# A two-layer diffusion block with sixteen experts: rotary query columns in one tile, earlier expert loads, and a first block of slots made from the counts alone

## What is computed

```
cq, ckv, kr, bq, bk, bv, dq, dk, dv, u = split_in(modulate(rms_norm(x)) @ w_in)
# MLA: 4 heads, a query is 64 plain and 32 rotary columns
qa = (rms_norm(cq) @ w_uq).reshape(B, L, 4, 64 + 32)
qa = concat([q_nope, apply_rope(q_rope)])              # latent tokens are roped, context tokens not
ka = concat([k_nope, broadcast(apply_rope(kr))])       # one rotary key for all heads
oa = softmax(qa @ ka * MLA_SCALE) @ va
ob = windowed softmax with a sink (bq, bk, bv)         # "swa"
oc = (softmax(dq1 @ dk1) - lam * softmax(dq2 @ dk2)) @ dv   # "diff"
od = means over 2/4/8/16 positions (u), times pool_w   # "pool"
x  = x + gate * rms_norm(concat(oa, ob, oc, od) @ w_out)
# experts: top-1 of 4 groups, top-2 of its 4 experts
h  = modulate(rms_norm(x)); e1, e2, w1, w2 = route(h @ router_gw, h @ router_ew)
x  = x + gate * rms_norm(sum_e w_e * (silu(h @ gate_e) * (h @ up_e)) @ down_e)
```

## Time and profile before

| | us |
|---|---|
| median of the runs | 1171.84 |
| the three runs | 1171.67, 1171.84, 1176.56 |
| the profiled execution's own time | 1174.54 |
| its span in the profile | 1172.7 |
| PE busy | 912.5 (78%) |
| DVE busy | 363.0 (31%) |
| ACT busy | 266.9 (23%) |
| POOL busy | 174.1 (15%) |

### The profile page before, as it was taken

One profiled execution on the slowest core, in us unless ns is written; L12 is line 12 of the kernel. 1 busy time (PEld: TensorE's weight loads), 2 busy tenths in 40 slices (PEclk: granted clock), 3 DMA queues, 4 the chain that ended last, 5 costly groups with the idle time before them and its releaser, 6 DMA issues. The chain is left out here.

```text
span 1172.7 us, 23091 instructions
## 1 busy us (share of the span) xinstructions
PE 912.5 (78%) x8840; PEld 570.6 (49%) x8841; DVE 363.0 (31%) x909; ACT 266.9 (23%) x728; POOL 174.1 (15%) x256
## 2 busy tenths in 40 slices
PE   3999998999995899989973399988994873764570
PEld 2454644556454566656642366746643542432240
DVE  1100057568335111111110664376624110100013
ACT  4121034556232011101100521035521000000001
POOL 0010015000021222112211230032012110100011
PEclk9999999999996899999997699999995998977796
DMA  9972334660357799999997995130068999999963
GB/s 377 347 262 101 144 144 148 231 234 1 137 187 306 258 412 409 410 411 411 411 411 296 386 345 205 33 125 31 8 251 316 404 408 410 410 411 410 410 272 139
DMA packets 97332, 323.03 MB, mean 275 GB/s; under 512 B 11946, under 2 KB 22964, under 8 KB 90996
## 3 DMA queue, kind: packets, MB, share of 16 engines
q1 hardware_dynamic: 70528, 279.19, 60.4%
q0 software_dynamic: 9600, 31.81, 7.8%
q10 hardware_dynamic: 17140, 11.13, 3.0%
HBM read 309.58 MB, written 18.81 MB: 280 GB/s over the span
## 5 line engine op out<-in xcount | busy, mean ns | idle before, releaser
L851 PE MATMUL psum<-weights,lat 128*32 128x256 f32 x2688 | 177.0, 418 | 99.3 <-DMA weights<-in_exp_w_gu_dram 61.9
L851 PEld LDWEIGHTS psum<-weights,lat 128*32 128x32 f32 x2688 | 107.5, 119 | 164.0 <-issue 130.7
L1662 DVE STREAM_TRANSPOSE lat<-lat 128x256 f32<-128x256 f32 x66 | 29.4, 446 | 352.3 <-PE psum L851 341.1
L529 PE MATMUL psum<-hT,weights 128*128 128x512 f32 (+1 forms) x336 | 121.1, 519 | 3.5 <-ACT lat L1025 1.9
L1201 ACT ACTIVATE lat<-psum 128x128 f32<-128x128 f32 x64 | 17.7, 277 | 356.0 <-PE psum L851 352.5
L529 PEld LDWEIGHTS psum<-hT,weights 128*128 128x128 f32 x336 | 64.4, 193 | 56.8 <-issue 48.4
L864 PE MATMUL psum<-weights,lat 128*32 128x256 f32 x1344 | 85.0, 391 | 5.4 <-issue 4.7
L1908 POOL DMA_INDIRECT lat<-h_rows,slot_col x68 | 66.5, 978 | 54.2 <-POOL slot_col L1905 52.2
L1433 DVE TENSOR_REDUCE st<-psum 128x1 f32<-128x512 f32 (+1 forms) x96 | 56.5, 599 | 41.5 <-PE psum L647 20.6
L864 PEld LDWEIGHTS psum<-weights,lat 128*32 128x32 f32 x1344 | 55.2, 114 | 27.0 <-issue 6.9
L1905 POOL COPY slot_col<-slots 128x1 int32 (+1 forms) x68 | 12.4, 183 | 364.3 <-DVE lat L1662 347.1
(11 more groups left out here) (269 smaller groups left out, 1226.6 us busy)
## 6 DMA issues: line engine op xcount, KB each, us to landing
weights<-in_exp_w_gu_dram SPq DMA_DIRECT2D x44, 2048.0 KB
weights<-in_ada_w_dram SPq DMA_DIRECT2D x24, 2048.0 KB, 8.5
weights<-in_exp_w_down_dram SPq DMA_DIRECT2D x22, 2048.0 KB
hT<-in_exp_w_gu_dram SPq DMA_DIRECT2D x10, 2048.0 KB
R<-in_exp_w_gu_dram SPq DMA_DIRECT2D x10, 2048.0 KB
spare_w<-in_exp_w_down_dram SPq DMA_DIRECT2D x10, 2048.0 KB
weights<-in_w_in_dram SPq DMA_DIRECT2D x6, 2048.0 KB, 15.0
weights<-in_w_out_dram SPq DMA_DIRECT2D x4, 2048.0 KB, 9.6
```

What stands on the lines that cost most here:

```text
L529: mm = nc.tensor.matmul(t[:, lo:hi], w[:, k, col:col + P], hT[:, k, lo:hi], start=(k == 0), stop=(k == KD - 1))
L851: mm = nc.tensor.matmul(gu_ps[BLK * j:BLK * j + BLK, 0:256], xgT[:, k, :], w[:, k % 4, j, :, :, :], start=(k == 0), stop=(k == KD - 1), sk ...
L1662: nc.vector.transpose(xgT[:, :, :].rearrange("p k s -> p (k s)"), xg[par]).then_inc(x_ready, 1)
```

## The change

Four things are changed.

1. The columns of `w_uq` are loaded in another order: the four heads' 64 plain columns side by side (two heads per tile, `qn`), and all heads' 32 rotary columns in one tile of 128 (`qr`). So PE makes three tiles of 128 columns instead of four of 96; one rotation, one product with cosines and one `rope` do for the four heads, with the constants of "diff" (same dimension); and the "mla" constants are gone (the constants' load shrinks from 3,265 to 2,629 columns). The load of `w_uq` becomes four DMAs, with pieces of 64 or 32 columns, 256 or 128 bytes, where one DMA had pieces of 1,536 bytes. ACT copies the parts of the tiles to the heads, and also takes over the four `kr` copies from DVE. The first scores wait for `qr_out` and `kr_out`.
2. In layer 0 `ROPED_LATE` has the units 4, 8, 12 and 16 instead of 3 to 6, and the split of the context half of `dq` (four copies with three heads zeroed) is done by ACT in `project`, so DVE's split has 256 columns instead of 512.
3. SP's loads of the first three experts: some pieces of experts 0 and 1 are issued during the mixing, as their places fall free (`bv` and `dk` change places in `W[0]` for that, and `dg` gets a buffer of its own in layer 1). Expert 2's `lo` now waits for the stored rows as well.
4. The first block's slots need no list: the tokens of expert 0 with rank 0 to 31 are found from "rk" alone (`hot0` on DVE, "s0" on PE, `slot_col` on DVE), and POOL issues gather 0 by it, ahead of its wait for `slots`.

The diff, cut to its core:

```diff
-        ROPED_LATE = {3: "dq0", 4: "dk0", 5: "dq1", 6: "dk1"}
+        ROPED_LATE = [{4: "dq0", 8: "dk0", 12: "dq1", 16: "dk1"}, {3: "dq0", 4: "dk0", 5: "dq1", 6: "dk1"}]
...
 # PE, latent_projections
-                for h in range(HEADS):
-                    t = take("qa", L, h)
+                for col, job in ((2 * P, ("qr", L)), (0, ("qn", L, 0)), (P, ("qn", L, 1))):
+                    t = take(*job)
                     for j in range(2):
-                        mm = nc.tensor.matmul(t[0:MLA_QK, 0:nq], w_uq[:, j, h * MLA_QK:(h + 1) * MLA_QK], cq[:, j, 0:nq],
-                                              start=(j == 0), stop=(j == 1))
+                        mm = nc.tensor.matmul(t[:, 0:nq], w_uq[:, j, col:col + P], cq[:, j, 0:nq], start=(j == 0), stop=(j == 1))
...
-                for name in ("qa0", "qa1", "qa2", "qa3"):
-                    x, kind, lo, hi = ROPES[L][name]
-                    rotate(S, L, name, x, kind, lo, hi)
+                x, kind, lo, hi = ROPES[L]["qr"]
+                rotate(S, L, "qr", x, kind, lo, hi)
...
 # PE, mix
-                            pe.wait_ge(*at("roped", L, f"qa{h}"))
+                            pe.wait_ge(*at("qr_out", L, h))
                             pe.wait_ge(*at("ka", L, h))
                             pe.wait_ge(*at("kr_out", L, h))
...
 # PE, route, between "rk" and "st"
+                pe.wait_ge(*at("hot0", L))
+                t = take("s0", L)
+                for i in range(nt):
+                    for a in range(QUADS):
+                        mm = nc.tensor.matmul(t[BLK * a:BLK * a + BLK, 0:4], hot0[:, i, :], ones[:, 0:4],
+                                              start=(i == 0), stop=(i == nt - 1), skip_group_check=True)
...
 # ACT's queue in layer 0, small_weights
-            eng.dma_start(w_uq[:, :, :], A["mla_w_uq"][L].rearrange("(j p) n -> p j n", p=P)).then_inc(*mark(S, by=16))
+            for j in range(2):
+                src = A["mla_w_uq"][L].rearrange("(j p) (h c) -> p j h c", p=P, h=HEADS)[:, j, :, :]
+                for at_col, lo, hi in ((0, 0, MLA_NOPE), (2 * P, MLA_NOPE, MLA_QK)):
+                    dst = w_uq[:, j, at_col:at_col + HEADS * (hi - lo)].rearrange("p (h c) -> p h c", h=HEADS)
+                    eng.dma_start(dst, src[:, :, lo:hi]).then_inc(*mark(S, by=16))
...
 # ACT, project
-                    copy(S, dqs[L][:, j, 0, 0:nq], (f"dq{j}", L), nq, scale=DIFF_SCALE, keys=[("tile", L, f"dq{j}")])
+                    src = read(act, f"dq{j}", L)
+                    for c in range(4 if nq > SEQ else 0):
+                        a(dqs[L][:, j, c, SEQ:nq], src[:, SEQ:nq], ACT.Copy, scale=C("quarter_scaled")[:, c:c + 1])
+                    copy(S, dqs[L][:, j, 0, 0:SEQ], (f"dq{j}", L), SEQ, scale=DIFF_SCALE, keys=[("tile", L, f"dq{j}")])
...
 # ACT, latent_projections
-                for h in range(HEADS):
-                    copy(S, qas[L][0:MLA_QK, h, 0:nq], ("qa", L, h), nq, hi=MLA_QK, scale=MLA_SCALE, keys=[("tile", L, f"qa{h}")])
+                src = read(act, "qr", L)
+                for h in range(HEADS if nq > SEQ else 0):
+                    a(qas[L][64:96, h, SEQ:nq], src[MLA_ROPE * h:MLA_ROPE * (h + 1), SEQ:nq], ACT.Copy, scale=MLA_SCALE)
+                a(qr[:, 0:SEQ], src[:, 0:SEQ], ACT.Copy, scale=MLA_SCALE).then_inc(*mark(S, ("read", "qr", L), ("tile", L, "qr")))
+                for j in range(2):
+                    src = read(act, "qn", L, j)
+                    for b in range(2):
+                        a(qas[L][0:MLA_NOPE, 2 * j + b, 0:nq], src[64 * b:64 * b + 64, 0:nq], ACT.Copy, scale=MLA_SCALE)
...
+                for name, dst, src in (("kr", kas[L], [kr[64:96, :]] * HEADS), ("qr", qas[L], [qr[MLA_ROPE * h:MLA_ROPE * (h + 1), 0:SEQ] for h in range(HEADS)])):
+                    act.wait_ge(*at("roped", L, name))
+                    for h in range(HEADS):
+                        a(dst[64:96, h, 0:src[h].shape[1]], src[h], ACT.Copy).then_inc(*mark(S, (name + "_out", L, h)))
...
 # DVE, route
+                tt_(rs[:, 38, 0:nt], C(f"token{L}")[:, 0:nt], chosen[:, 0:nt], ALU.mult).then_inc(*mark(S, ("token0", L)))
...
                 t = read(v, "rk", L)
+                step(tt_(hot0[:, 0:nt, :], t[:, 0:nt].unsqueeze(2).to_broadcast([P, nt, BLK]),
+                         C("count")[:, 0:BLK].unsqueeze(1).to_broadcast([P, nt, BLK]), ALU.is_equal))
+                v.wait_ge(*at("token0", L))
+                step(tt_(hot0[:, 0:nt, :], hot0[:, 0:nt, :], rs[:, 38, 0:nt].unsqueeze(2).to_broadcast([P, nt, BLK]), ALU.mult), ("hot0", L))
...
                 step(nc.vector.tensor_tensor_scan(start32[:, :], ones[:, 0:17], nb32[:, :], 0.0, ALU.mult, ALU.add))
+                first = read(v, "s0", L)
+                ts(slot_col[:, 0:1], first[:, 0:1], C("quad"), None, ALU.add).then_inc(*mark(S, ("read", "s0", L), ("slot0", L)))
...
 # SP, ahead of a layer's experts
-                sp.wait_ge(*at("filled", "o", L, len(units(L)) - 1))
+                last, per = len(units(L)) - 1, len(units(L)) // 3
+                if L:
+                    sp.wait_ge(*at("used", item_no[("ada", 1, 11)]))
+                    load_piece(L, 1, 1, "hi")
+                sp.wait_ge(*at("filled", "o", L, per - 1))
+                load_piece(L, 0, 0, "lo")
+                sp.wait_ge(*at("filled", "o", L, 2 * per - 1))
+                load_piece(L, 0, 0, "hi")
+                if L == 0:
+                    sp.wait_ge(*at("filled", "s", L, last, 1))
+                    load_piece(L, 1, 1, "dn")
+                sp.wait_ge(*at("filled", "o", L, last))
                 sp.wait_ge(*at("filled", "pool", L, 1))
-                for piece in PIECES:
-                    load_piece(L, 0, 0, piece)
+                load_piece(L, 0, 0, "dn")
                 for n in (hi - 2, hi - 1):
                     sp.wait_ge(*at("used", n))
-                for piece in PIECES:
+                for piece in (("lo", "dn") if L else ("lo", "hi")):
                     load_piece(L, 1, 1, piece)
                 sp.wait_ge(*at("filled", "lg", L, tiles(L) - 1))
-                load_piece(L, 2, 2, "lo")
                 for tt in range(tiles(L)):
                     sp.wait_ge(*at("h_stored", L, tt))
+                load_piece(L, 2, 2, "lo")
```

67 lines of the change are left out of this document (40 added, 27 removed).

## The result

The changed kernel ran in 1167.77 us (median; 1161.24 to 1170.35), the kernel before, beside it, in 1173.86 (1171.15 to 1176.56). The ratio is 0.9946, 95% interval 0.9932 to 0.996: faster by 0.5%, some 6 us, where 11.2 us, 1.0%, had been forecast. The profiled execution took 1167.77 us, its span in the profile is 1165.9 us.

What follows compares the result with a forecast made beforehand. DMA engines bound the expert stages, where only the stream's start counts; elsewhere the PE, DVE, ACT chain does. Terms 1.8 − 6.0 − 1.3 − 1.9 − 3.8 = −11.2 from the median 1171.84 gave 1160.6 us, range 1154.5 to 1169.5.

Steps and rivals of the forecast that it cites:

- (a): Layer 0's load of w_uq: its small pieces on ACT's queue delay ACT by 5.4 us; cost +1.8 us, bounds 0 and +4.1.
- (b): Layer 0's mixing: PE's idles of 1.40 and 3.67 us and the slow clock behind go; −6.0 us, bounds −2 and −8.
- the mixing gives most of it back: Rival: gap before first scores lowers the clock, ACT's copies delay first units; (b) and (d) shrink to about −3; chance 0.24.
- (d): Start of layer 1's mixing: DVE takes first maxima at 774.0 instead of 775.96; −1.9 us, bounds 0 and −3.
- (c): Layer 0's handover: early gather 0 lets the first block and the saturated stream start earlier; −1.3 us, bounds −0.5 and −1.6.
- (e): Layer 1's handover: store and gathers land sooner, expert 2's hi and dn go out earlier; −3.8 us, bounds 0 and −5.
- (f): Early loads of expert pieces during the mixing: worth 0 by themselves, counting only through (e).
- Slower: Rival: w_uq's small pieces pass ACT's queue at only 60 per us, PE late by 26.3 us; net +13.3, 1185; chance 0.05.
- the store isn't held by the load: Rival, layer 1's handover: engines serve queues in turn, so moving lo doesn't help; (e) only −1.5, total −8.9, 1163.0; chance 0.08.

## Why the prediction was right or wrong

**What bounds the kernel**: right. The share of the DMA engines stayed at 1.02 to 1.03 and 407 GB/s in both expert stages, and what counted was when they begin.

**(a) +1.8**: the time right, in part by luck. At the squares it is 1.8 us between the means of the two kernels' two traces each, with PE's wait at 0.5 to 2.35. But ACT's delay, which I took as 5.4 us against a slack of 3.6, is 3.6 in the mean over all traces; only the earlier trace rows, whose first copy at 59.50 is one of the earliest, makes it 5 to 6, and the second trace of the kernel before has that copy at 62.92 and 0.75 us of wait already. So delay and slack were both put too high. The pace was better than the 232 small packets per us that I took: 320. By the prediction's estimate from the price of small transfers in the Trainium skill ("DMA: Bandwidth & Descriptors", section "Why small descriptors are slow") the term would be nothing; the traces disagree, since what the pieces held was the issuing queue.

**(b) −6.0**: wrong, and this is where the forecast failed. Measured: 229.61 and 231.07 before, 230.87 and 228.39 after, 0.7 us of gain by these two pairs. Two steps failed. First, "the change halves the steps and puts them eight units apart, so one split (about 1.9 us) no longer fills the lead": the width was not what made the split long. I read 3.58 us from the earlier trace rows as the price of 2,048 columns and halved it, though POOL's busy time of 3.61 us stood in the earlier trace rows beside it. With half the columns, fully beside the pooling means, it took 4.42; without POOL, 1.27. Half the columns alone would have taken only 0.5 us off (1.80 to 1.27), not 1.7. The stall of 3.67 became one of 2.56 at another place. Second, the gap ahead of the first scores, which I had put at 2.7 us and which is 2.90: I counted its slow stretch as a risk in the bounds, not in the sum, though the earlier trace rows shows just that behind a wait of 3.67. It came in both traces: from the first scores to the first turn it took 8.72 and 7.23 us for 7.04, although the 1.40 of idle in it was gone; at the full clock it takes 5.59. That the first scores themselves would come no earlier was right: 100.7 and 100.8 us behind the squares before, 100.9 twice after. The rival "the mixing gives most of it back" is what happened, (b) and (d) together −3.2 for its −3; its reason, ACT's copies, is one part (moving the `kr` copies back gave some 4 us), and POOL, which it didn't name, the other (5 to 6 us).

**(c) −1.3**: the size nearly right (32.65 and 32.73 to 31.61 and 32.08, −0.85), the cause wrong. I gave it to the early gather; the experiment without it lost 0.2 us at x_turn, the one without early loads 1.3 there and the whole gain at the stream (32.89). In the kernel before, layer 0's last store ran beside `lo` and what stood before it and took 8.1 us; in the changed kernel it took 4.2, without the early loads 8.0, and the gathers wait for it. My reading of the earlier trace rows as layer 0's last store, taking 2.9 us, hid this: the handover of layer 0 had the same fault as layer 1's.

**(d) −1.9**: right, and for its reason. Counted from the rotation of `kr`, the first scores stand where they were (14.1 us before, 14.0 after, now with the gap of 2.90 ahead of them), and the first maxima come at 15.13 us instead of 17.1, in both pairs, since DVE is free for them. By `w_out` it is 85.32 and 84.45 to 82.85 and 81.88, −2.5.

**(e) −3.8**: right: 16.87 and 16.90 to 13.14 and 12.52, −4.1. By its steps, counted from the store's issue (890.40 in the forecast, 891.00 in the trace): the store landed after 4.5 us, where 3.1 had been forecast; the list's last step ended after 8.6, as forecast; gather 1 went out after 9.6 for 10.0, and `hi` after 13.1, as forecast. Undoing `lo`'s place costs 1.6 to 2.2, undoing the early gather 1.2 to 1.8, undoing the early loads all of it.

**(f) 0**: wrong as a term, since it is the condition of (c) and (e): without the early loads the others give nothing. In (e) I had counted two pieces instead of three, so the sum doesn't miss it, but whoever had judged the early loads by (f) would have left them out. What they would give alone, in the kernel before, no run shows.

The measured terms, +1.8 − 0.7 − 0.85 − 2.5 − 4.1, make −6.4, near the 6.1 and 8.4 us between the medians in the two comparisons. That is not a closed account: the terms are read from four traces whose spans differ by 9.3 us in the mean. Of the 2.9 us that are left, 1.8 are the slow issue on ACT's queue at the end, a gain that the forecast didn't have and whose cause is open; the rest is spread over stretches that vary with the clock. "Slower" didn't come: at 320 small packets per us the queue was never near the 60 of that case. The rival "the store isn't held by the load" is refuted by the run with `lo` first.

## What to carry to other kernels

Before halving the duration of a VectorE step, look at what GpSimd does beside it; a wait that lets GpSimd start a little later can be worth more than a narrower step. A short latency-bound DMA (a store that is gathered from right after) wants the loads ahead of it thinned out; loads moved early into idle stretches pay there, and not where they are waited for. Work handed to an engine that is idle on average still lands on the path where that engine is the last one before a stage begins; and the idle of TensorE that it makes can be paid once more in what follows at the lower clock (here behind the gap of 2.90 us in eight traces of nine).

## What the runs showed of the hardware that I had not expected

Four DVE steps of 128x256 (one input and one output in SBUF, a scalar per partition) took 1.27 us alone, 1.65 where one of them met a single POOL product of 0.71 us, 2.9 beside POOL operations of 0.6 to 0.8 us in layer 1, and 4.42 beside operations of 1.1 to 1.3 us. Four of 128x512 took 1.80 alone and 3.58 beside POOL's. So 256 columns more cost 0.13 us a step, and one meeting with POOL up to 1.1. A store of 512 KB takes 2.9 us with the DMA engines free, 3.8 to 4.7 behind the end of two 2 MB loads, 7.8 to 8.9 beside loads in flight. Some 320 small packets per us went through beside large loads, more than the 232 that the kernel before had asked for. After 2.9 us of idle PE its next two products took 2.08 us for 1.02, at a granted clock of 0.50, so at 1.2 instead of 2.4 GHz; in the run without early loads the same gap left the clock at 1.00 and they took 1.12. Issuing one of ACT's last stores took 1.5 to 1.8 us, for 0.32 of its neighbours, in all four traces of kernels built on the one before, and in none of the other ten.
